# Modulation chunks ahead of the experts: four sets, each adding into one PSUM bank, and the second layer's experts behind the read-back

## The chip, the core and the metric

The kernel runs on one core of one Trainium2 chip. The metric is the device time in microseconds (us). All data is float32. Weights lie in HBM (main memory) and come over the core's 16 DMA engines.

## What is computed

Two layers over 384 tokens of 1024 elements (128 context tokens, 256 latent tokens), cut to what matters:

```python
for l in range(2):
    # 6 vectors of 1024 elements for each of two conditioning vectors (c_ctx, c)
    sh1, sc1, g1, sh2, sc2, g2 = (silu(cond) @ ada_w[l] + ada_b[l]).split(6)   # ada_w[l]: 1024 x 6144
    h = rms_norm(x, norm_mix_g[l]) * (1 + sc1) + sh1
    x = x + g1 * (attention(h) if l == 0 else multi_scale_pool(h))
    h = rms_norm(x, norm_ffn_g[l]) * (1 + sc2) + sh2
    x = x + g2 * moe(h)        # 32 experts, 2 for each token; 3 MB of weights each
```

The six modulation vectors of a layer depend on the conditioning vectors alone, not on x: `ada_w` can be multiplied at any time. It is 24 MB a layer, 48 MB in all. The experts are 96 MB a layer.

## The kernel before

**Engines and queues.** Each engine runs a list of instructions in the order in which it is written, and waits on semaphores. SP (SyncE) issues nearly all loads, in order: a wait on SP holds back every load behind it. PE multiplies, ACT and DVE move results out of PSUM (8 banks of 128 x 512 floats, the accumulators of PE), POOL gathers and scatters token rows with indirect DMAs.

**Modulation.** `ada_w` comes as 24 chunks of 2 MB, 12 a layer, each for 512 of a layer's 6144 columns. For a chunk i, `ada(i)` (line 1254) multiplies the two conditioning vectors by it, in 8 matmuls of 32 stationary columns and 512 moving ones (line 1266), four beside each other in the array; the result stands as rows in bank i % 2. `ada_copy(i)` (ACT, line 634) copies the bank to `adas`. `ada_vectors(i)` (PE, line 1270) turns these rows into columns with 4 small matmuls (line 1276) into bank 2, from where DVE's `modulation` adds the bias and makes the scales. So each chunk costs PE a product, and a turn that needs a copy between. Chunks 0 to 3 come at the head, 4 to 9 between the nine qkv products (line 1342), 10 to 15 (`LATE`) around the router of layer 0, 16 to 19 (`BETWEEN`) after the experts of layer 0, 20 to 23 around the router of layer 1.

**Attention** (lines 1373 to 1440) runs in 28 steps over 24 units. In step u PE makes the scores of unit u (1382), at some steps the product with the values of four units (1399), and the transposes of the probabilities of unit u - 2 (1410, 1417), which wait until DVE has copied those of unit u - 3; ACT takes exponentials (687), DVE the row maxima (949), the scaling (958) and the copies (968). From step 19 on the output projection (1438) runs along.

**Router and experts.** `norm_pe` (1455), the router's logits (1474), the tokens turned to rows (1493), and a long chain of small DVE instructions with small matmuls between, which ends in two tables: the first (1537) gives the indices by which POOL gathers rows, the second (1550) the weights. Then 32 tiles of 64 rows run, one for each expert, and in layer 0 one more tile for an expert with more rows. `rows_T` (1571), `gate_up` (1595), `hidden_T` (1604) and `down` (1619) are PE's work of a tile. The weights of four experts have a place in `ring`, those of a fifth (`more_gu`, `more_down`) in other buffers. The load for a later expert into a place waits until the tile that held it is through (`gu_mm`, `down_mm`). After the last tile of layer 0 its results are read back from HBM (503), added to x, pooled and multiplied (1691, 1731), and layer 1 goes on with its norm and router.

**Places of chunks.** Three places (TAIL, LEFT, RIGHT) are used in turn, two more are where `wo` goes later (HIGH0, HIGH1). Chunks 16 to 23 use places of the ring as well, so the experts of layer 1 are loaded as these chunks are multiplied. LEFT and RIGHT lie in `adaw`, whose first part is the tiles' gathered rows: POOL clears it (line 531) when chunk 14 is multiplied.

Of the kernel before, what the change touches and what calls it, by code (L numbers as in the profile page):

```python
# [26 lines left out]
ALU = mybir.AluOpType  # L27
# [3 lines left out]
P = 128  # L31
# [27 lines left out]
for _name, _w in (("ident", P), ("ones", P), ("upper", P), ("sel2", 2), ("assign", 6), ("eps", 1), ("column_sum", 1),  # L59
# [11 lines left out]
def constants():  # L71
# [10 lines left out]
    put("sel2", (p % 32) == np.arange(2)[None, :])  # L82
# [50 lines left out]
def build(nc, x_prompt, x_sample, c, cache_k, cache_v, c_ctx, norm_mix_g, norm_ffn_g, ada_w, ada_b,  # L133
# [3 lines left out]
    with ExitStack() as ctx:  # L137
# [19 lines left out]
        condT = sb("condT", [P, KD, 32])  # L157
# [40 lines left out]
        ada_place += [ring[:, 0, 0:KD * ACH], ring[:, 1, 0:KD * ACH]]  # L198
        TAIL, LEFT, RIGHT, HIGH0, HIGH1, SLOT0, SLOT1, SPLIT = range(8)
        ADA_AT = [TAIL, LEFT, RIGHT, HIGH0, HIGH1] + [(i + 2) % 3 for i in range(5, 16)]  # L200
        ADA_AT += [SLOT0, SLOT1, RIGHT, SPLIT, HIGH0, HIGH1, RIGHT, RIGHT]
# [36 lines left out]
        split = [xT[:, :, :].rearrange("p k t -> p (k t)"), flat_h[:, 2 * D:3 * D]]  # L238

        def ada_weights(i):  # L240
            if ADA_AT[i] == SPLIT:
                return [split[k // 6][:, k % 6 * ACH:(k % 6 + 1) * ACH] for k in range(KD)]
            return [ada_place[ADA_AT[i]][:, k * ACH:(k + 1) * ACH] for k in range(KD)]

# [15 lines left out]
        s_adaw = [sem(f"s_adaw{i}") for i in range(8)]  # L260
# [72 lines left out]
        LATE = AFTER_QKV[6] + 1  # L333
        BETWEEN = LATE + 6
# [8 lines left out]
        MODS_STEP = 5  # L343
        WO_STEPS = {19 + d: d for d in range(KD)}
        WO_BANKS = (2, 7)
# [14 lines left out]
        def ada_bank(i):  # L360

            return bank[i % 2]

# [7 lines left out]
        def _(sp):  # L371
            def load_ada(i):
                if ADA_PRIOR[i] >= 0:
                    sp.wait_ge(ada_mm, ADA_PRIOR[i] + 1)
                w = ada_w[i // NCH, i % NCH]
                if ADA_AT[i] == SPLIT:
                    sp.dma_start(split[0], w[:, 0:6 * ACH]).then_inc(s_adaw[SPLIT], 16)
                    sp.dma_start(split[1], w[:, 6 * ACH:]).then_inc(s_adaw[SPLIT], 16)
                else:
                    sp.dma_start(ada_place[ADA_AT[i]], w).then_inc(s_adaw[ADA_AT[i]], 16)  # L380
# [1391 lines left out]
```

## Time and profile before

| | |
|---|---|
| median of 3 runs | 904.78 us (903.8 to 907.23) |
| the profiled execution | 905.74 us, of which 903.7 us are its span, first to last instruction |
| PE busy | 751.9 us (83%) |
| DVE, ACT, POOL busy | 356.5, 151.8, 174.9 us |
| chunk products (line 1266) | 208 matmul rows, 28.4 us busy on PE in all |
| moved from HBM | 294.35 MB, mean 326 GB/s |
| granted TensorE clock | 0.937 of 2.4 GHz on average |

The page of the profile splits the span in 40 slices of 22.6 us and gives for each the busy share of every engine in tenths, the granted clock of PE and the share of the DMA engines. The chain is the work that ended last, followed back from the end. In the timeline the number in brackets is how long the engine sat idle before a row, and what ended it. A matmul on float32 is two passes, so 8 matmuls stand as x16.

### The profile page before, as it was taken

The numbers are of one execution on the slowest core, as the hardware profiler recorded it, in microseconds if no ns is written. First come the engines' busy times: TensorE is split into PE (matmuls) and PEld (weight loads), VectorE is DVE, ScalarE is ACT, GpSimd is POOL, SyncE is SP. The second block draws the span as 40 slices with busy tenths as digits, with TensorE's granted clock in tenths as the row PEclk, the third lists the DMA queues.
The fourth block names the chain that finished last, engine by engine and source line by source line (L and its number), as shares of the span: only waits on it lengthen the run. The fifth ranks groups of instructions, "written<-read, shape, count | busy, mean of one in ns | idle before, by whom it ended". The sixth has DMA issues, their size and how long they took to land.

```text
span 903.7 us, 13190 instructions
## 1 busy us (share of the span) xinstructions
PE 751.9 (83%) x4704; PEld 425.8 (47%) x4704; DVE 356.5 (39%) x834; ACT 151.8 (17%) x360; POOL 174.9 (19%) x275
## 2 busy tenths in 40 slices
PE   4999977899889999877787885986999988877860
PEld 3544543478456554444444534544655544444430
DVE  2221448732463434333333334455244423333333
ACT  3211155520431100000000013442010000000000
POOL 0000400000003333322333210002134333322220
PEclk9999969999989999999999988985999999999995
DMA  9998700005886999999999988986599999999925
GB/s 345 428 433 378 211 1 12 1 1 232 354 318 265 386 410 418 422 422 419 422 421 420 389 373 326 387 341 253 213 403 378 423 422 422 420 424 421 414 91 209
DMA packets 39384, 294.35 MB, mean 326 GB/s; under 512 B 10584, under 2 KB 12048, under 8 KB 19376
## 3 DMA queue, kind: packets, MB, share of 16 engines
q1 hardware_dynamic: 26656, 275.50, 74.4%
q0 software_dynamic: 10880, 13.26, 4.8%
q10 hardware_dynamic: 1808, 5.06, 1.4%
q8 instruction: 25, 0.41, 0.2%
q14 instruction: 15, 0.12, 0.0%
HBM read 293.23 MB, written 22.02 MB: 349 GB/s over the span
## 4 chain that ended last, share of the span: by engine, by line
PE 59%; DMA 28%; DVE 6%; issue 3%; ACT 2%; SPq 1%; POOL 0%; ACTq 0%; POOLq 0%; DVEq 0%
DMA ring<-in_moe_w_in 22%; PE bank L1595 18%; PE bank L1619 8%; PE bank L1342 7%; PE bank L1266 4%; PE bank L1438 3%; PE bank L1571 3%; PE bank L1276 2%; DMA adaw<-results 2%; PE bank L1446 2%; PE bank L1474 2%; PE bank L1399 1%; PE bank L1455 1%; DMA adaw<-in_ada_w 1%; PE bank L1731 1%
## 5 line engine op out<-in xcount | busy, mean ns | idle before, releaser
L1595 PE MATMUL bank<-ring,qkv 128*64 128x256 f32 x2016 | 247.0, 399 | 61.1 <-issue 39.1
L1595 PEld LDWEIGHTS bank<-ring,qkv 128*64 128x64 f32 x2016 | 161.0, 143 | 129.3 <-issue 70.4
L1121 DVE COPY qkv<-bank 128x512 f32<-128x512 f32 x64 | 44.3, 692 | 224.7 <-PE bank L1571 224.7
L553 POOL DMA_INDIRECT results<-adaw,scur x65 | 67.6, 1040 | 315.0 <-DVE adaw L1144 280.3
L1619 PE MATMUL bank<-ring,qkv 128*64 128x512 f32 x504 | 122.0, 604 | 1.2 <-DVE qkv L1133 0.8
L816 ACT ACTIVATE qkv<-bank 128x128 f32<-128x128 f32 x64 | 17.8, 278 | 441.6 <-PE bank L1595 441.6
L543 POOL DMA_INDIRECT adaw<-rows,gcur x57 | 59.1, 1036 | 44.3 <-POOL gcur L540 44.3
L1342 PE MATMUL bank<-ring,hT 128*128 128x512 f32 x144 | 63.7, 596 | 1.3 <-DVE hT L891 1.3
L1619 PEld LDWEIGHTS bank<-ring,qkv 128*64 128x64 f32 x504 | 31.0, 136 | 47.5 <-issue 45.6
L1144 DVE SCALAR_TENSOR_TENSOR adaw<-bank,wcur,adaw 128x512 f32<-128x512 f32 x64 | 48.1, 751 | 2.3
L1142 DVE SCALAR_TENSOR_TENSOR adaw<-qkv,wcur 128x512 f32<-128x512 f32 x64 | 48.1, 751 | 2.3
L1133 DVE COPY qkv<-bank 128x128 f32<-128x128 f32 x64 | 18.7, 292 | 76.7 <-PE bank L1604 76.7
L1571 PE MATMUL bank<-con,adaw 128*128 128x128 f32 x260 | 43.1, 289 | 5.1 <-DMA adaw<-rows,gidx 3.2
L1342 PEld LDWEIGHTS bank<-ring,hT 128*128 128x128 f32 x144 | 26.7, 190 | 32.8 <-issue 31.6
L1571 PEld LDWEIGHTS bank<-con,adaw 128*128 128x128 f32 x260 | 27.6, 142 | 30.0 <-issue 30.0
L531 POOL MEMSET adaw<- 128x2048 f32 x2 | 3.6, 1804 | 194.3 <-PE bank L1266 161.8
L1604 PEld LDWEIGHTS bank<-con,qkv 128*128 128x128 f32 x64 | 9.0, 141 | 52.7 <-DVE qkv L1127 51.1
L1266 PE MATMUL bank<-adaw,condT 128*32 128x512 f32 x208 | 28.4, 669 | 2.5 <-DMA adaw<-in_ada_w 2.5
L1276 PEld LDWEIGHTS bank<-con,adas 128*128 128x128 f32 x192 | 23.1, 192 | 13.9 <-issue 13.9
L687 ACT ACTIVATE ring<-bank,ss 128x384 f32<-128x384 f32 (+1 forms) x48 | 24.0, 506 | 32.3 <-DVE ss L949 32.2
L1438 PE MATMUL bank<-hT,ring 128*128 128x256 f32 x128 | 29.1, 380 | 0.0
L1438 PEld LDWEIGHTS bank<-hT,ring 128*128 128x128 f32 x128 | 23.7, 190 | 3.7 <-DVE xT L979 0.8
(231 smaller groups left out, 764.0 us busy)
## 6 DMA issues: line engine op xcount, KB each, us to landing
ring<-in_moe_w_in SPq DMA_DIRECT2D x63, 2048.0 KB, 24.5
ring<-in_moe_w_out SPq DMA_DIRECT2D x63, 1024.0 KB, 20.4
adaw<-in_ada_w SPq DMA_DIRECT2D x13, 2048.0 KB, 18.2
ring<-in_ada_w SPq DMA_DIRECT2D x10, 2048.0 KB, 20.9
ring<-in_attn_w_qkv SPq DMA_DIRECT2D x3, 2048.0 KB, 35.7
ring<-in_attn_w_o SPq DMA_DIRECT2D x1, 4096.0 KB, 22.9
adaw<-in_moe_w_in SPq DMA_DIRECT2D x2, 2048.0 KB, 7.8
adaw<-results SPq DMA_DIRECT2D x8, 512.0 KB, 6.1
```

The source lines that it names most:

```text
L543: pool.indirect_dma_start(xg[:, b], None, rows, bass.IndirectOffsetOnAxis(ap=gcur[:, b:b + 1], axis=0), bounds_check=row_limit, oob_is_err ...
L553: pool.indirect_dma_start(res, bass.IndirectOffsetOnAxis(ap=scur[:, p, :], axis=0), yout[:, p], None, bounds_check=res_limit, oob_is_err=F ...
L1121: V.tensor_copy(xgT[:, p], bank[2][:, :]).then_inc(xgT_ready, 1)
L1142: V.scalar_tensor_tensor(yout[:, p], gdiff, wcur[:, p, 1:2], glat, ALU.mult, ALU.add).then_inc(y_order, 1)
L1144: V.scalar_tensor_tensor(yout[:, p], bank[4 + p % 2][:, :], wcur[:, p, 0:1], yout[:, p], ALU.mult, ALU.mult)\
L1266: last = T.matmul(out[32 * j:32 * j + 32, :], condT[:, k, :], w[k], start=half == 0, stop=half == 1, skip_group_check=True)
L1276: last = T.matmul(bank[2][:, at:at + 2], adas[:, i % 4, j * P:(j + 1) * P], C("sel2"), start=True, stop=True)
L1342: last = T.matmul(bank[5 + g % 3][:, :], hT[:, k, t * P:(t + 1) * P], wqkv[n][:, k, :], start=k == 0, stop=k == KD - 1)
L1438: last = T.matmul(bank[WO_BANKS[d % 2]][:, 0:NTOK - CTX], wo[:, k, d * P:(d + 1) * P], hT[:, k, CTX:NTOK], start=k == 0, stop=k == KD - 1)
L1571: last = T.transpose(bank[2][:, i * P:(i + 1) * P], xg[:, q, i * P:(i + 1) * P], ident)
L1595: last = T.matmul(bank[p][64 * a:64 * a + 64, 0:2 * P], xk[:, k % 4, k // 4], w[:, :, k, a * P:(a + 1) * P], start=k == 0, stop=k == KD - ...
L1619: last = T.matmul(bank[4 + p][64 * a:64 * a + 64, :], hidT[:, p, 64 * j:64 * j + 64], w[j][:, a * 512:(a + 1) * 512], start=j == 0, stop=j ...
```

## The change

- The 24 chunks are cut into four sets, `SETS = (0, 4, 10, 19, 24)`. All chunks of a set add into one bank: the two conditioning columns stand in columns 30 and 31 of a buffer 62 wide that is otherwise zero, and chunk number m of a set multiplies the 32 columns from 30 - 2m on, so its result lands in rows 2m and 2m + 1 and the other rows add zero. One copy and one group of 4 turning matmuls then serve a whole set (`set_copy`, `vectors`) in place of one for each chunk.
- Chunk 10 moves to just ahead of attention, chunks 11 to 18 into attention at steps 2, 3, 4, 5, 9, 12, 13 and 16 (`ADA_STEPS`), each between the scores and the transposes. Chunks 19 to 23 stay around the router of layer 0. No chunk is left in layer 1, nor between the layers.
- SP loads chunks 8 to 21 in one row as places come free, and 22 and 23 behind the third expert of layer 0. After layer 0 it issues the read-back at once, and behind it the four ring experts of layer 1 with no wait between.
- POOL clears `adaw` when chunk 20 is multiplied. `modulation` and the scales are split; `MODS_STEP` is 4 instead of 5; the two banks of the output projection change places, and its second product waits for `set_copy(2)`.

```diff
+        ADA_AT = [TAIL, LEFT, RIGHT, HIGH0, HIGH1] + [(i + 2) % 3 for i in range(5, 22)] + [TAIL, RIGHT]
...
+        SETS = (0, 4, 10, 19, 2 * NCH)
+        SET_BANK, VECTOR_BANK = (0, 1, 2, 0), (2, 0, 2, 2)
...
+        ADA_STEPS = {2: 11, 3: 12, 4: 13, 5: 14, 9: 15, 12: 16, 13: 17, 16: 18}
...
-        MODS_STEP = 5
+        MODS_STEP = 4
...
-            for i in range(8, LATE + 3):
+            for i in range(8, 22):
                 load_ada(i)
...
-                    for i in range(LATE + 3, BETWEEN):
-                        load_ada(i)
-                    sp.wait_ge(ada_mm, LATE + 4)
+                    load_ada(22)
+                    load_ada(23)
+                    sp.wait_ge(ada_mm, 23)
                     load_expert(l, 3)
...
                     sp.wait_ge(extras_over, 1)
-                    load_ada(BETWEEN + 4)
-                    load_ada(BETWEEN + 5)
-                    for b in range(2):
-                        sp.wait_ge(ada_mm, BETWEEN + b + 1)
+                    for b in range(RING):
                         load_expert(l, b)
                     sp.wait_ge(x_sum, TT)
-                    load_ada(BETWEEN + 6)
-                    sp.wait_ge(ada_mm, BETWEEN + 6)
-                    load_expert(l, 2)
-                    load_expert(l, 3)
-                    load_ada(BETWEEN + 7)
-                    sp.wait_ge(ada_mm, 2 * NCH)
-                    sp.wait_ge(ada_vec, 2 * NCH - 2)
...
-                    pool.wait_ge(ada_mm, BETWEEN - 1)
+                    pool.wait_ge(ada_mm, 21)
...
+            def set_copy(n):
+
+                act.wait_ge(ada_mm, SETS[n + 1])
+                A.activation(adas[:, n, :], bank[SET_BANK[n]][:, :], ACT.Copy).then_inc(ada_copied, 1)
...
             def ada(i):
 
+                n = set_of(i)
+                c = 30 - 2 * (i - SETS[n])
...
-                        last = T.matmul(out[32 * j:32 * j + 32, :], condT[:, k, :], w[k],
-                                        start=half == 0, stop=half == 1, skip_group_check=True)
+                        last = T.matmul(out[32 * j:32 * j + 32, :], condT[:, k, c:c + 32], w[:, k],
+                                        start=i == SETS[n] and half == 0, stop=i + 1 == SETS[n + 1] and half == 1,
+                                        skip_group_check=True)
...
+            def vectors(n):
+
+                pe.wait_ge(ada_copied, n + 1)
+                a, b = SETS[n], SETS[n + 1]
+                out = bank[VECTOR_BANK[n]][:, 8 * a:8 * b].rearrange("p (c j x) -> p j c x", j=4, x=2)
+                for j in range(4):
+                    last = T.matmul(out[:, j], adas[:, n, j * P:(j + 1) * P],
+                                    C("sel")[:, 0:2 * (b - a)].rearrange("p (c x) -> p c x", x=2), start=True, stop=True)
                 last.then_inc(ada_vec, 1)
...
+            vectors(1)
+            ada(10)
             pe.wait_ge(qk_copied, 4)
             pe.wait_ge(k_copied, 3)
-            pe.wait_ge(ada_copied, LATE)
...
+                if u in ADA_STEPS:
+                    ada(ADA_STEPS[u])
...
-                    ada(LATE)
-                    ada(LATE + 1)
-                else:
-                    ada(BETWEEN + 4)
-                    ada(BETWEEN + 5)
-                    ada_vectors(BETWEEN + 4)
-                    ada_vectors(BETWEEN + 5)
+                    vectors(2)
+                    ada(19)
+                    ada(20)
...
-                    ada(BETWEEN)
-                    ada(BETWEEN + 1)
-                    ada_vectors(BETWEEN)
-                    ada_vectors(BETWEEN + 1)
-                    ada(BETWEEN + 2)
-                    ada(BETWEEN + 3)
                     pe.wait_ge(mods_ready, 4)
-                    ada_vectors(BETWEEN + 2)
-                    ada_vectors(BETWEEN + 3)
```

How the instructions move. On PE, from a qkv product to the first attention steps, the kernel before has (1266 is a chunk product, 1276 its turn, 1328 the turns of queries and keys, 1382 scores, 1410 and 1417 transposes):

```order
L1342 MATMUL bank<-ring,hT 128x512 x8
L1266 MATMUL bank<-adaw,condT 32x512 x8
L1276 MATMUL bank<-con,adas 128x2 x4
L1328 MATMUL bank<-con,qkv 128x128 x8
L1342 MATMUL bank<-ring,hT 128x512 x8
L1276 MATMUL bank<-con,adas 128x2 x4
L1342 MATMUL bank<-ring,hT 128x512 x8
L1328 MATMUL bank<-con,qkv 128x128 x2
L1328 MATMUL bank<-con,ring 128x128 x2
L1328 MATMUL bank<-con,qkv 128x128 x10
L1382 MATMUL bank<-ring 128x384 x6
L1410 MATMUL bank<-con,ring 128x128 x4
```

The same place in the changed kernel, where line 1216 is the chunk product, 1227 the turn of a set, 1291 the qkv product, 1277 the turns of queries and keys, 1331 the scores:

```order
L1291 MATMUL bank<-ring,hT 128x512 x8
L1216 MATMUL bank<-adaw,condT 32x512 x8
L1277 MATMUL bank<-con,qkv 128x128 x8
L1291 MATMUL bank<-ring,hT 128x512 x16
L1277 MATMUL bank<-con,qkv 128x128 x2
L1277 MATMUL bank<-con,ring 128x128 x2
L1277 MATMUL bank<-con,qkv 128x128 x10
L1227 MATMUL bank<-con,adas 128x6x2 x4
L1216 MATMUL bank<-ring,condT 32x512 x8
L1331 MATMUL bank<-ring 128x384 x6
L1216 MATMUL bank<-adaw,condT 32x512 x8
L1361 MATMUL bank<-con,ring 128x128 x4
```

The turns between the qkv products are gone; one turn and chunk 10 stand ahead of the first scores, and a chunk between scores and transposes. On PE, from the norm of layer 1 (1455) to the first tile (1571), the kernel before has:

```order
L1455 MATMUL bank<-qkv,con 128x384 x8
L1266 MATMUL bank<-ring,condT 32x512 x16
L1276 MATMUL bank<-con,adas 128x2 x8
L1474 MATMUL bank<-hT,wr 36x384 x8
L1478 MATMUL bank<-con,rt 128x36 x3
L1266 MATMUL bank<-adaw,condT 32x512 x8
L1493 MATMUL bank<-con,hT 128x128 x16
...
L1276 MATMUL bank<-con,adas 128x2 x4
L1537 MATMUL bank<-hT 128x43 x6
L1276 MATMUL bank<-con,adas 128x2 x4
L1550 MATMUL bank<-hT 128x43 x6
L1571 MATMUL bank<-con,adaw 128x128 x4
```

The changed kernel there (1407 is its norm, 1422 its logits, 1477 and 1484 its tables, 1507 its first rows):

```order
L1407 MATMUL bank<-qkv,con 128x384 x8
L1422 MATMUL bank<-hT,wr 36x384 x8
L1426 MATMUL bank<-con,rt 128x36 x3
L1437 MATMUL bank<-con,hT 128x128 x16
...
L1477 MATMUL bank<-hT 128x43 x6
L1484 MATMUL bank<-hT 128x43 x6
L1507 MATMUL bank<-con,adaw 128x128 x4
```

All four chunks and their turns have left this place. On SP, around the read-back (503), the kernel before issues:

```order
L380 DMA ring<-in_ada_w 128x4096
L380 DMA adaw<-in_ada_w 128x4096
L377 DMA xT<-in_ada_w 128x3072
L378 DMA hT<-in_ada_w 128x1024
L503 DMA adaw<-results 128x1024 x4
L503 DMA qkv<-results 128x1024 x2
L380 DMA ring<-in_ada_w 128x4096 x2
L383 DMA ring<-in_moe_w_in 128x4096
L387 DMA ring<-in_moe_w_out 128x2048
```

and the changed one, where line 467 is the read-back and 370 and 374 are the expert loads:

```order
L467 DMA adaw<-results 128x1024 x4
L467 DMA qkv<-results 128x1024 x2
L370 DMA ring<-in_moe_w_in 128x4096
L374 DMA ring<-in_moe_w_out 128x2048
L370 DMA ring<-in_moe_w_in 128x4096
```

The chunk loads ahead of and behind the read-back are gone, and the expert loads follow it.

## Rows read from the trace of the kernel before

**Rows 1.** The page, 40 slices: granted PE clock and DMA share in tenths

```profile
PEclk9999969999989999999999988985999999999995
DMA  9998700005886999999999988986599999999925
```

**Rows 2.** Window of layer 0's tiles: length; busy PE, PEld, DVE, ACT, POOL; clock, DMA, GB/s

```profile
352.00:520.00 168.00, 136.11 (x939) 77.07 (x937) 57.41 (x124) 5.66 (x21) 50.26 (x82) 0.98 1.01 417
```

**Rows 3.** The chain that ended last, head and qkv products: start, length, what

```profile
33.43 1.89 PE bank L1276 x16
...
59.52 1.85 PE bank L1266 x16
61.37 0.98 PE bank L1276 x8
...
69.33 1.85 PE bank L1266 x16
```

**Rows 4.** The chain, attention: first exponential, first values, first output projection

```profile
126.42 1.24 ACT ring L687 x4
...
143.84 2.93 PE bank L1399 x12
...
182.11 3.52 PE bank L1438 x16
```

**Rows 5.** Timeline of PE in attention: start, length, idle before it in brackets

```profile
130.76 1.65 PE L1382 MATMUL bank<-ring 64*128 64x384 f32 x4
...
135.80 0.92 PE L1382 MATMUL bank<-ring 64*128 64x384 f32 x4
...
174.67 0.63 PE L1410 MATMUL bank<-con,ring 128*128 128x128 f32 x4 [1.38 <-DVE ring L968]
```

**Rows 6.** Windows, columns as in the window above

```profile
160.00:182.00 22.00, 17.85 (x107) 9.39 (x105) 16.72 (x42) 13.45 (x46) 0.00 (x0) 1.00 0.00 1
585.00:591.00 6.00, 5.62 (x49) 2.80 (x48) 3.35 (x4) 1.72 (x3) 0.00 (x0) 1.00 0.30 68
592.00:602.00 10.00, 8.62 (x23) 2.70 (x27) 5.46 (x17) 5.15 (x9) 0.00 (x0) 0.69 1.01 430
```

**Rows 7.** The chain, layer 0 from its last norm product to its first tile

```profile
234.42 1.58 PE bank L1455 x4
...
241.18 5.82 PE bank L1474 x16
...
264.27 2.79 PE bank L1537 x12
267.06 3.57 PE bank L1266 x16
...
276.72 0.47 PE bank L1571 x4
```

**Rows 8.** The chain, last scatter of layer 0, then that of layer 1

```profile
540.03 6.25 DMA results<-adaw,scur
...
877.43 2.83 DMA results<-adaw,scur
```

**Rows 9.** The chain, layer 1 from its norm to its first tile

```profile
585.18 3.57 PE bank L1266 x32
...
592.80 8.00 PE bank L1474 x16
...
603.65 11.04 DMA adaw<-in_ada_w
...
619.57 1.39 PE bank L1537 x12
...
622.57 6.62 DMA adaw<-rows,gidx
```

**Rows 10.** DMA issues: count, median us from issue to landing

```profile
adaw<-rows,gidx POOLq DMA_INDIRECT x8, 3.8
```

**Rows 11.** Timeline of DVE, router of layer 1: what the first table waits for

```profile
616.90 1.62 DVE L1073 TENSOR_SCALAR hT<-con,rt 128x128 f32<-128x128 f32 x6
```

More of the change, by code:

```diff
@@ L197, in build @@
                      high[:, 0:KD * ACH], high[:, KD * ACH:KD * D]]
[L198 to L201, printed above, removed]
+        TAIL, LEFT, RIGHT, HIGH0, HIGH1 = range(5)
+        ADA_AT = [TAIL, LEFT, RIGHT, HIGH0, HIGH1] + [(i + 2) % 3 for i in range(5, 22)] + [TAIL, RIGHT]
         ADA_USE = [ADA_AT[:i + 1].count(ADA_AT[i]) for i in range(2 * NCH)]
@@ L235, in build, with set_of @@
         flat_h = hT[:, :, :].rearrange("p k t -> p (k t)")
[L238 to L243, printed above, removed]
+        SETS = (0, 4, 10, 19, 2 * NCH)
+        SET_BANK, VECTOR_BANK = (0, 1, 2, 0), (2, 0, 2, 2)
+        def set_of(i):
+            return sum(i >= first for first in SETS) - 1
         more_gu = cc[:, 4096:8192]
@@ L259, in build @@
         s_wqkv = [sem(f"s_wqkv{n}") for n in range(3)]
-        s_adaw = [sem(f"s_adaw{i}") for i in range(8)]
+        s_adaw = [sem(f"s_adaw{i}") for i in range(5)]
         pool_order, dve_order = sem("pool_order"), sem("dve_order")
@@ L620, in _ @@
             for i in range(2):
[L621 removed]
+                A.activation(condT[:, :, 30 + i], gains[:, 40 + 8 * i:48 + 8 * i], ACT.Silu).then_inc(cond_ready, 1)
             act.wait_ge(s_const, 16)
@@ L757, in raw @@
                             .then_inc(xt_copied, 1)
-                    for i in range(BETWEEN, BETWEEN + 4):
-                        ada_copy(i)
                     square(0)
@@ L807, in keep @@
                     A.activation(xtok[:, t, q * 512:(q + 1) * 512], bank[6 + n % 2][:, :], ACT.Copy).then_inc(x1_copied, 1)
-                for i in (range(LATE + 3, BETWEEN) if l == 0 else (BETWEEN + 7,)):
-                    ada_copy(i)
+                if l == 0:
+                    set_copy(3)
                 def silu(s, p, old=True):
@@ L870, in _, with modulation, scales @@
             dve.wait_ge(rows_read, 3)
[L872 to L874 removed]
+            def modulation(n, l, a, b):
+                cols = bank[VECTOR_BANK[n]][:, l * 2 * NMOD + 2 * a * KD:l * 2 * NMOD + 2 * b * KD]
                 m = mods[:, l, a * KD:b * KD, :]
[L876 to L886 removed]
+                order(V.tensor_tensor(m, cols.rearrange("p (m c) -> p m c", c=2),
+                                      bias[:, l, a * KD:b * KD].unsqueeze(2).to_broadcast([P, (b - a) * KD, 2]), ALU.add))
+            def scales(l, i, first):
+                m = mods[:, l, i * KD:(i + 1) * KD, :]
+                order(V.tensor_scalar(m, m, 1.0, None, ALU.add))
+                order(V.tensor_tensor(m, m, gains[:, first:first + KD].unsqueeze(2).to_broadcast([P, KD, 2]), ALU.mult))
+            dve.wait_ge(ada_vec, 1)
+            modulation(0, 0, 0, 2)
+            scales(0, 1, 0)
             V.memset(ss[:, 15:16], 0.0).then_inc(mods_ready, 1)
@@ L972, in _ @@
                 if u == MODS_STEP:
-                    dve.wait_ge(ada_vec, LATE)
-                    modulation(0, 2, 5)
+                    dve.wait_ge(ada_vec, 2)
+                    modulation(1, 0, 2, 5)
+                    scales(0, 4, 16)
                     V.memset(ss[:, 16:17], 0.0).then_inc(mods_ready, 1)
```

157 lines of the change are left out of this document (42 added, 115 removed).

## The prediction

> **What bounds the kernel now.** I read the page first: PE's clock and the DMA share in 40 slices [rows 1]. The DMA engines stand at 9 tenths in the two long stretches of expert tiles and at 0 from 113 to 203 us, which is attention. The window over most of layer 0's tiles [rows 2] shows 1.01 of DMA share at 417 GB/s, with PE busy 136 of 168 us: the tiles are bound by weights. Five experts are loaded ahead in each layer, the load of the sixth waits for the first tile's gate_up, and from there 27 experts of 3 MB follow each other. So the end of a stretch of tiles is the start of its first gate_up plus a fixed stream, and the change leaves this stream as it is. What can change the time lies outside: the head, qkv, attention, the two routers, and the passage between the layers. The 16 MB that layer 1 no longer loads are worth nothing by themselves, since its five experts wait loaded for the first tile in both kernels. I went through the chain in these parts, then the timelines for what stands beside it. All times below are against the profiled execution, 905.74 us with a span of 903.7; its run is 0.96 above the median of 904.78.
>
> **Head and qkv.** At the head the chunks' turns go from four groups to one. PE's chunks, transposes of x and turns stand end to end; in the order of the new kernel one turn of 0.98 is left behind chunk 3 and its copy. By the old rows the two last groups took 1.89 [rows 3], an earlier one 0.98; against this the last copy is now exposed for 0.7 or so. I take 1.8 off (bounds 0, if the first qkv weights land no earlier than now, and 2.2). Between the qkv products six turns of 0.98 go: the pitch from one chunk to the next is 9.81, of which the chunk is 1.85 and the turn 0.98 [rows 3], and what is left is the product. That is 5.9 off, as long as chunk loads keep up; the DMA share falls under 9 tenths from the fourth slice on, 68 us [rows 1], so the queue runs dry while the products go on. Sum: 7.7 earlier at the end of qkv. A rule of the Trainium skill speaks against the moves further on (TensorEngine Tiling, Key Properties): changing the tiling mode drains TensorE, and each chunk in attention adds two changes between 32-column and full matmuls. The row leaves nothing for it here: 59.52 + 1.85 = 61.37 and 61.37 + 0.98 = 62.35, to the hundredth the next start. By the rule each of 16 changes would cost something; by the row the sum is unchanged.
>
> **Ahead of attention.** One turn and chunk 10 now stand between the last transposes of keys and the first scores, with nothing to hide them. The clock is at its half level there: scores of one unit took 1.65 at 130.76 and 0.92 at 135.80 [rows 5]. A chunk takes 1.85 at full and 3.57 at half clock [rows 3, 7]. I take 1.1 + 3.6 = 4.7. As PE is then busy without a break from the transposes on, I expect the full clock back by the first scores, so that they take half as long and the first exponential comes 5.0 earlier than the old 126.42 [rows 4], a loss of 2.7 of the 7.7 (bounds 1.0 and 4.7).
>
> **Chunks 11 to 14** (steps 2 to 5). The old kernel takes 17.4 from the first exponential to the first product with values at 143.84 [rows 4], partly at half clock, and with a pause in PE while DVE normalizes the context queries at step 3. At full clock a step with a chunk is 0.92 of scores, 1.85, and about 0.8 of transposes (0.63 and the third key tile's [rows 5]), 3.6 in all. After 1.2 of exponential and 0.9 of scores three such steps take 10.8, and DVE, which by then is in its normalization, needs about 5 more for that and two steps: 17.9. A chunk of 2 MB takes 5 us at 417 GB/s [rows 2] and some to start, so chunk 14, whose place is free only after chunk 11, would be just in time. With some of it at half clock I take a loss of 1.5 (bounds 0 and 7).
>
> **Chunks 15 to 18.** Here PE is busy 17.85 of 22 us with three of the chunks to come, 5.6 us of work [rows 6], so at least 1.4 is lost there if every gap serves. Gaps ahead of transposes like the 1.38 at 174.67 [rows 5] do serve: there PE waits for DVE's copy. Step by step I find 0.8 for chunk 15, 1.5 for 16 and 17, 0.4 for 18: 2.7 (bounds 1.4 and 7.4). The output projection, at 182.11 in the old chain [rows 4], then starts at -7.7 + 2.7 + 1.5 + 2.7 = **-0.8** against before. If all ends sit at their bounds, -5.7 and +13.2.
>
> **Router of layer 0.** The two chunks and the one turn behind the norm are hidden as now, under 5.2 us of DVE and ACT from 236.00 to 241.18 [rows 7]. One turn on each side of chunk 21 goes, but DVE's marks bound the counting matmuls: 1.25 earlier. The first table comes at 263.0 instead of 264.27 and takes 2.79 at half clock [rows 7]. Then one chunk of up to 3.57, the second table of 1.39 to 2.79 [rows 7, 9], one turn of 1.0, and 0.5 of DVE; old: two chunks and four turns. First rows at 272.4 to 273.8 for the old 276.72 [rows 7]. POOL's clearing, which the old kernel could only do after chunk 14, is out of the way; the gather lands by 271 at its median of 3.8 [rows 10]. I take **-3.4** (bounds -2.2 and -4.8).
>
> **Between the layers.** The last scatter of layer 0 takes 6.25 with four chunk loads in the queues, that of layer 1, with no load about, 2.83 [rows 8]. The read-back is issued behind it, so **-3.4** (bounds 0 and -3.8). The chunks between hid under scatter and read-back and cost nothing; their products kept PE at work, though, see below. I add **+0.5** for a longer stay at half clock.
>
> **Layer 1.** From the last norm product, 585.18, to the logits at 592.80 are 7.6 [rows 9]; in layer 0 the same norm takes 5.2, as there DVE has no modulation to wait for. So -2.4. The wait of 11.04 for a chunk's weights [rows 9] looks like the big gain and is not: the first table at 619.57 needs DVE's six marks, the last of which ends at 618.52 [rows 9, 11]. Only the 1.05 between go, and about 1.3 of matmuls at half clock may; against this the table itself may take 2.79 instead of 1.39. I take -0.8. The gather of 6.62 [rows 9] runs against the fifth expert's load, which now comes long before: 3.8 by its median [rows 10], -2.8. Together **-6.0** (bounds -3.5 and -7.8). The tiles and the tail follow unchanged.
>
> **Sum.** -0.8 - 3.4 - 3.4 + 0.5 - 6.0 = -13.1: 905.74 - 13.1 = 892.6 for the profiled execution, and 0.96 less for the median, **891.7 us**.
>
> **Rivals.**
> - *Attention pays each chunk in full* (chance 0.12). For it: PE is the busiest engine there, 17.85 of 22 [rows 6]. Against: the gaps. Price: 8 x 1.85 = 14.8 and 4.7 ahead, so -7.7 + 4.7 + 14.8 = +11.8 at the output projection, 12.6 more than forecast: 904.3, no change.
> - *Half clock through attention* (0.04): slower. The place is steps 2 to 16. For it: in 585 to 591 PE was busy 5.62 of 6 us, all chunks and turns, and yet the stretch from 592 ran at 0.69 [rows 6], so chunks may not hold the clock. Against: in 160 to 182 it was 1.00 [rows 6], with the same scores and transposes. Price: 8 x 3.57 = 28.6 and 4.7, so +25.6, 26.4 more than forecast: 918. It decides where the loss ahead of and in attention is over 24.5 (the 7.7 before it, the 12.3 behind it, and 4.5): less 4.7, that is 2.5 for each chunk.
> - *PE cold behind the read-back* (0.12). Without chunks PE rests some 16 us, and the window products, pool products and logits start at half clock; the logits already took 8.00 instead of 5.82 [rows 7, 9]. The logits lost 2.2 by it; if the window and pool products, each of such a length, lose as much and half as much again, the passage is 6.6 longer: 898.3. The Trainium skill puts it as a rule (TensorE: Matmul & The Clock Gate, The HAM clock gate): the throttled state is the default, and activity releases it. Against: 5 us after a product at half clock the next was at full [rows 5].
> - *Everything serves* (0.14): the chunks keep the clock full in attention and sit in gaps (-3.5 at the output projection), routers at their far bounds (-4.8, -7.8), scatter -3.8: -19.9 and 0.96, 884.9.
> - *The forecast* has 0.58.
>
> **Numbers.** The kernel's runs spread 0.4%, so 0.5%, 4.5 us, is about what can be told from no change. Slower by more needs over 909.3: the half clock, and a loss in attention with one at layer 1 beside it, 0.05. Within: 900.3 to 909.3, most of the first rival and a third of the cold-PE case, 0.13. Faster: 0.82. The range: below 884 nothing but the far bounds together, above 900 the first two rivals, so 884 to 900 leaves out about 0.2.
>
> **What would show it.** Chain: output projection within 3 us of 182; first layer-0 gate_up near 274; last scatter of layer 0 under 3.5 us; logits of layer 1 at 5.2 us behind the norm; its first gather near 4; no idle PE on chunk weights in attention. Total time of the two tile stretches equal to before. The prediction is wrong if attention grows over 15 us, if a chunk load is late at steps 4 to 9, or if the tiles of either layer take longer because their loads now start otherwise.

## The result, and the profile after

The changed kernel takes 893.0 us (median of 4 executions, 889.83 to 893.44), the kernel before beside it 906.0 (median of 4): a ratio of 0.985, 95% interval 0.9816 to 0.9884. Forecast were 891.7 us and "faster" with 0.82. In a second round of runs it was 891.3 against 902.8 (0.9877, 0.9851 to 0.9903). The profiled execution of after is the fastest, 889.83, so the two profiled ones differ by 15.9 and the medians by 13.0; where the other 3 may lie is said below.

The page of after: busy times, granted clock and DMA share, as in [rows 1].

```profile
PE 726.6 (82%) x4544; PEld 404.4 (46%) x4544; DVE 356.0 (40%) x830; ACT 140.8 (16%) x340; POOL 175.4 (20%) x275
...
PEclk9999999999977999999999996985999999999995
DMA  9999858714868899999999947923699999999935
```

The chain that ended last, with the places of [rows 3, 4]:

```profile
3.70 27.67 DMA ring<-in_ada_w
31.41 1.97 PE bank L1216 x16
...
59.33 1.85 PE bank L1216 x16
61.18 7.06 PE bank L1291 x16
68.25 1.85 PE bank L1216 x16
...
116.76 3.51 PE bank L1216 x16
120.27 0.87 PE bank L1331 x4
...
122.16 1.24 ACT ring L648 x4
...
140.08 2.80 PE bank L1350 x12
...
180.65 3.46 PE bank L1390 x16
```

Each matmul stands as two rows (x16 for 8); that these are its two passes, as said ahead, no run shows. The turn between chunk and product is gone: the pitch is 8.92 for 9.81. The first two rows are why the head gave nothing: the load ahead of chunk 3 lands at 31.37 and the chunk is multiplied at once, so what went from TensorE before that had lain under the load. Chunk 10, at 116.76, runs at half clock, the scores behind it at full. The output projection starts 1.46 earlier than in [rows 4].

The same chain from layer 0's norm to its first tile, for [rows 7]:

```profile
232.89 1.58 PE bank L1407 x4
...
240.94 5.34 PE bank L1422 x16
...
252.81 2.45 PE bank L1446 x12
...
264.70 2.79 PE bank L1477 x12
...
276.34 3.67 PE bank L1531 x15
```

The norm ends 1.5 earlier than before, the logits (240.94) start 0.24 earlier and the first table 0.43 later. Two windows say why. First VectorE and GpSimd there (start, length, engine, line):

```profile
239.17 1.63 DVE L960 TENSOR_SCALAR hT<-hT,mods 128x128 f32<-128x128 f32 x1
239.43 1.37 DVE L958 TENSOR_TENSOR hT<-xT,qkv 128x384 f32<-128x384 f32 x1
239.89 0.97 DVE L960 TENSOR_SCALAR hT<-hT,mods 128x128 f32<-128x128 f32 x1
```

```profile
238.91 1.80 POOL L495 MEMSET adaw<- 128x2048 f32 x1 [133.76 <-PE bank L1216]
```

GpSimd clears xg as soon as chunk 20 is multiplied, and VectorE's steps beside it take 1.63 and 1.37 in place of 0.34 and 0.55. All end with it: 240.80, 240.80 and 240.86 for 240.71. Before, the clearing ran at 270.72. Then windows, with the columns of [rows 6] (the granted clock is the third number from the end):

```profile
248.00:252.00 4.00, 3.07 (x27) 1.74 (x20) 3.48 (x17) 1.93 (x2) 0.00 (x0) 1.00 0.49 123
252.00:256.00 4.00, 3.52 (x24) 3.20 (x22) 0.94 (x6) 1.92 (x2) 0.00 (x0) 0.65 1.06 390
256.00:260.00 4.00, 4.00 (x22) 2.35 (x24) 1.28 (x7) 2.86 (x3) 0.00 (x0) 0.50 0.79 313
```

TensorE is at 0.65 in the window from 252 and at its half level behind it, and the counts at 252.81 take 2.45 (1.53 at the full level, in a run below). The kernel before had the full level there, and up to 260:

```profile
252.00:256.00 4.00, 3.08 (x27) 2.60 (x25) 1.33 (x6) 3.31 (x4) 0.00 (x0) 1.00 0.76 299
```

Between the layers and in layer 1, for [rows 8, 9]:

```profile
534.30 2.37 DMA results<-adaw,scur
...
538.51 6.78 DMA adaw<-results
...
548.55 2.61 PE bank L1619 x10
...
575.14 1.57 PE bank L1407 x4
...
581.91 8.21 PE bank L1422 x16
...
607.71 2.80 PE bank L1477 x12
...
617.43 4.75 PE bank L1531 x21
```

The scatter takes 2.37 for 6.25, the logits stand 5.2 behind the norm for 7.6, the gather is no longer in the chain, and layer 1's first tile starts 13.8 earlier (617.43 for 631.26).

### The profile page after: what moved, and what is told of

It is laid out like the page before. It is cut to its first block, busy times and chain, and to the rows that moved or that the text cites. A ratio compares the mean times of both kernels' runs of the same rounds, so it can differ in the third digit from the quotient of the medians.

```text
span 887.8 us, 12796 instructions
## 1 busy us (share of the span) xinstructions
PE 726.6 (82%) x4544; PEld 404.4 (46%) x4544; DVE 356.0 (40%) x830; ACT 140.8 (16%) x340; POOL 175.4 (20%) x275
## 4 chain that ended last, share of the span: by engine, by line
PE 57%; DMA 28%; DVE 7%; issue 4%; SPq 1%; ACT 1%; POOL 0%; POOLq 0%; DVEq 0%
DMA ring<-in_moe_w_in 22%; PE bank L1531 17%; PE bank L1555 8%; PE bank L1291 7%; PE bank L1216 3%; PE bank L1390 3%; DMA ring<-in_ada_w 3%; PE bank L1507 3%; DMA adaw<-results 2%; PE bank L1398 2%; PE bank L1422 2%; PE bank L1350 1%; PE bank L1331 1%; PE bank L1407 1%; PE bank L1659 1%
## 5 line engine op out<-in xcount | busy, mean ns | idle before, releaser
L1531 PE MATMUL bank<-ring,qkv 128*64 128x256 f32 x2016 | 241.5, 393 | 63.1 <-issue 39.7
L1531 PEld LDWEIGHTS bank<-ring,qkv 128*64 128x64 f32 x2016 | 157.1, 141 | 129.7 <-issue 66.6
L1555 PEld LDWEIGHTS bank<-ring,qkv 128*64 128x64 f32 x504 | 31.0, 136 | 47.5 <-issue 45.6
L1291 PEld LDWEIGHTS bank<-ring,hT 128*128 128x128 f32 x144 | 26.8, 190 | 36.7 <-issue 35.5
L1216 PE MATMUL bank<-adaw,condT 128*32 128x512 f32 x240 | 30.2, 623 | 0.0
L1540 PE MATMUL bank<-con,qkv 128*128 128x128 f32 x64 | 21.2, 331 | 2.0 <-DVE qkv L1083 2.0
## 6 DMA issues: line engine op xcount, KB each, us to landing
adaw<-in_ada_w SPq DMA_DIRECT2D x15, 2048.0 KB, 11.6
```

The costliest lines, as they stand in the source:

```text
L1216: last = T.matmul(out[32 * j:32 * j + 32, :], condT[:, k, c:c + 32], w[:, k], start=i == SETS[n] and half == 0, stop=i + 1 == SETS[n + 1] ...
L1291: last = T.matmul(bank[5 + g % 3][:, :], hT[:, k, t * P:(t + 1) * P], wqkv[n][:, k, :], start=k == 0, stop=k == KD - 1)
L1531: last = T.matmul(bank[p][64 * a:64 * a + 64, 0:2 * P], xk[:, k % 4, k // 4], w[:, :, k, a * P:(a + 1) * P], start=k == 0, stop=k == KD - ...
L1540: T.transpose(bank[3][:, 0:P], hid[:, p], ident).then_inc(hid_mm, 1)
L1555: last = T.matmul(bank[4 + p][64 * a:64 * a + 64, :], hidT[:, p, 64 * j:64 * j + 64], w[j][:, a * 512:(a + 1) * 512], start=j == 0, stop=j ...
```

## The experiments

All are edits of the changed kernel. My theory A was: the gain is the six turns in qkv, the scatter and read-back without chunk loads, and layer 1's norm and gather; layer 0's router gave nothing because of the clearing and the clock. The rivals stand in each expectation. Ratios are to the kernel before, run beside each.

**The clearing, later** (`e1_clear_late`)

```diff
                     pool.wait_ge(s_out, 32)
+                    pool.wait_ge(slots_ready, 6)
```

> The changed kernel, with GpSimd's clearing of xg in layer 0 (1.80 us at 238.91 in its profile, beside the norm's VectorE work) held until the first six masks of the router are ready (about 264.5), where VectorE waits for TensorE's table. Theory A, the clearing slows VectorE's norm: the rstd step falls from 1.37 to about 0.6 us and the step behind it from 0.97 to 0.35, the logits start 1.2 to 1.4 earlier against the end of the norm's products (now 6.45 behind them), and the time is 1 to 1.4 us shorter. Rival B, the logits are late because of the set's vectors and chunks 19 and 20 ahead of them on TensorE: nothing moves, within 0.3 us. Rival C, the late clearing delays the first gather of layer 0: the first product of layer 0 starts up to 1.8 us later and the time is 0.5 to 2 us longer.

Measured: 890.8 us, 0.9839 (0.981 to 0.9868). Of its chain:

```profile
232.55 1.58 PE bank L1408 x4
...
239.31 5.82 PE bank L1423 x16
...
263.04 2.79 PE bank L1478 x12
```

The logits stand 5.18 behind the end of the norm's products for 6.47, so 1.3 came back as A says. This holds in every profile: 6.5 in all six with the clearing beside the norm, 5.2 in all six with it elsewhere. But a VectorE step of three elements a partition now stands beside the clearing, which ran from 263.13 to 264.93:

```profile
263.09 1.87 DVE L1033 TENSOR_SCALAR rt<-rt 128x3 f32<-128x3 f32 x1
```

That hides under the table's 2.79. From the table to the first tile it takes 12.28 for 11.64, with the set's turns at 1.45 for 1.30 and chunk 23 at 3.57 for 3.24; but with the clearing early this stretch took 11.26 to 13.3 in six profiles, so the 0.6 is not shown to be the clearing's. The first tile starts 0.7 earlier, counted from the first qkv product, in place of 1.3, and 0.3 earlier than in the second profile of the changed kernel. In the time of the kernel that is not to be told from nothing.

**Six groups of turns back between the qkv products** (`e2_turns_back`)

```diff
+                if g - 1 in AFTER_QKV:
+                    for j in range(4):
+                        T.matmul(bank[0][:, 400:402], adas[:, 0, j * P:(j + 1) * P], C("sel")[:, 0:2], start=True, stop=True)
```

> The changed kernel, with a group of four matrix products of 128x128 weights by two columns put back behind each of six query, key and value products, where the kernel before had the chunks' turns (they write a spare place, so nothing else changes). Theory A, the turns themselves cost what the query, key and value stage gave: that stage's end moves from 111.65 to 116.7 to 117.3, the time is 5.0 to 5.9 us longer. Rival B, that stage follows the landing of its loads and the turns were beside it: under 1 us longer. Rival C, half of the price lay in the copy from PSUM that each turn waited for: 2 to 4 us longer, since here no copy is waited for.

Measured: 898.1 us, 0.992 (0.9895 to 0.9944), 7.3 above the run with the late clearing beside it (up to 1.3 of this can be that clearing). Of its chain:

```profile
70.47 1.85 PE bank L1216 x16
72.32 0.98 PE bank L1303 x8
73.31 6.97 PE bank L1291 x16
80.28 1.85 PE bank L1216 x16
...
123.45 1.85 PE bank L1216 x16
...
127.19 1.24 ACT ring L648 x4
```

The pitch is 9.81 again, to the hundredth that of [rows 3], with no copy waited for: A holds, and B and C fall. The end of qkv is 6.7 later (118.3). Of that 5.35 are the six turns. The rest is mostly a stretch at a lower clock in the first products, ahead of the first of these turns: the first two groups of products took 15.67 for 13.97, with 0.67 granted from 38 to 42. Such a stretch comes and goes with the execution: from the first product to the end of qkv, 75.2 us passed in both profiles of the changed kernel and in three of the variants, and 76.9 to 78.1 in six others with the same code up to there. Unexpected: chunk 10 took 1.85, not 3.51, so only 5.0 is left at the first exponential. What the time has beyond that can be such variation too: layer 0's last gate product took 5.38 here and 3.70 in the changed kernel.

**The eight chunks in attention over 64 of 512 columns** (`e3_narrow_chunks`; it leaves out the rest of their product)

```diff
+                cols = 64 if 11 <= i < 19 else ACH
...
-                        last = T.matmul(out[32 * j:32 * j + 32, :], condT[:, k, c:c + 32], w[:, k],
+                        last = T.matmul(out[32 * j:32 * j + 32, 0:cols], condT[:, k, c:c + 32], w[:, k, 0:cols],
```

> The changed kernel, with the eight chunks inside the attention (11 to 18) multiplied over 64 of their 512 columns only (it leaves out the rest of their product, so layer 1's modulation is not the reference's); their loads stay. From the first exponential to the output projection it took 58.3 us in both profiles of the changed kernel. Theory A, the eight chunks cost the attention 2.3 to 3.5 us and the rest of their 14.8 us is hidden: that stretch takes 54.8 to 56. Rival B, they are all on the path: it takes 45 to 47. Rival C, they are all hidden, and what the attention lost is the clock at its start: it stays at 58. The first exponential itself stays where it is in all three, since chunk 10 is whole.

Measured: 894.3 us, 0.9844 (0.9806 to 0.9883), not faster. From the first exponential to the output projection 57.5 us pass for 58.5. Windows and timeline of this execution:

```profile
130.00:140.00 10.00, 7.25 (x98) 3.98 (x96) 9.76 (x19) 4.06 (x15) 0.00 (x0) 1.00 1.00 411
140.00:150.00 10.00, 8.19 (x28) 3.29 (x28) 5.85 (x17) 4.06 (x14) 0.00 (x0) 0.66 1.01 433
```

```profile
139.51 0.43 PE L1217 MATMUL bank<-adaw,condT 128*32 128x64 f32 x16 [2.20 <-DMA adaw<-in_ada_w]
```

A narrow chunk takes 0.43, so eight give back 11.4 us of TensorE, and the stretch gives 1.0. Other bounds take over: chunk 14 waits 2.20 for its load, VectorE is busy 9.76 of 10, and behind that wait the clock stands at 0.66 (1.00 in the same ten us of the changed kernel, counted from the first exponential), so that the first values product takes 4.81 for 2.80. With these 2.0 taken off, the chunks cost 3.0, inside A's range, but that is worked out and not seen: of the three, the run rules out only B. What it shows by itself is that removing most of the chunks' work won 1.0 us here and nothing that the time of the kernel shows. Against the expectation the first exponential moved too, 13.15 behind qkv for 10.54, in code that the edit leaves alone.

**Layer 1's fifth expert as late as before** (`e4_fifth_late`)

```diff
                     sp.wait_ge(x_sum, TT)
+                    sp.wait_ge(tab_mm, 3)
```

> The changed kernel, with the fifth expert's load of layer 1 held until the first table is multiplied, about where the kernel before issued it, so that it lands beside the first gather. Theory A, the gather was slow because of this load: it takes 6 to 7 us again from its issue to landing, the first product of layer 1 is 2 to 3 us later, and so is the end. Rival B, the gather is shorter in the changed kernel since there are no chunk loads and turns around it: under 0.5 us. Rival C, the later load is itself late for its tile (the fifth), as the queue has nothing ahead: up to 4 us more than A, with a wait for s_more in the fifth tile.

Measured: 894.0 us, 0.9894 (0.9864 to 0.9925), 3.2 above the run with the late clearing beside it, which again can hold up to 1.3 of that clearing. Of its chain:

```profile
611.87 6.70 DMA adaw<-rows,gidx
...
620.64 5.75 PE bank L1532 x32
```

The gather is 6.70, as the 6.62 of [rows 9], and the first tile starts at 620.64 for 617.43. In the changed kernel the gather is issued at 612.12 and the rows are multiplied at 615.70 without a wait, so there it took at most 3.6. A holds: the fifth expert's load makes the gather slow, with no chunk about.

**Chunk loads back ahead of the read-back** (`e5_loads_ahead`, and the same kernel again, `e5_ahead_again`, for its trace)

```diff
+                if l == 0:
+                    sp.wait_ge(gu_mm, LAST[0] + 1)
+                    sp.dma_start(ring[:, 0, 0:KD * ACH], ada_w[1, 8]).then_inc(s_ahead[0], 16)
...
+                    sp.dma_start(ada_place[RIGHT], ada_w[1, 10]).then_inc(s_ahead[2], 16)
...
+                    for n in range(3):
+                        sp.wait_ge(s_ahead[n], USED[n] + 16)
                 sp.wait_ge(results_in, l + 1)
```

> The changed kernel, with four chunk-sized loads put back ahead of the read-back of layer 0, at the places and behind the waits that the kernel before had, and multiplied by nobody. The read-back waits for three of them. Theory A, the last scatter and the read-back were slow because of these loads: the last scatter takes 5.5 to 6.5 us again in place of 2.37, the first window product is 3.5 to 5 us later, and the time is 3.5 to 5 us longer. Rival B, the scatter was slow in one execution only: under 1 us. Rival C, what cost the time before was the four chunks' products and their turns ahead of the windows on TensorE: then the loads alone give under 1.5 us.

> The kernel with four chunk-sized loads put back ahead of the read-back, again, for its trace. Its time was 896.3 us before. Theory A, scatter and read-back are slowed by the loads: last scatter 5.5 to 6.5 us in place of 2.4, the first window product 3 to 5 us later after the end of layer 0's tiles. Rival B, the scatter is short and the tiles of layer 0 are longer instead, as their own weights share the queue: tiles of layer 0 from first gate product to their end over 256 us in place of 255.3.

Measured: 896.3 us (0.9904, 0.9872 to 0.9936) and 895.6 us (0.992, 0.9895 to 0.9945), the second 4.3 above the changed kernel beside it. Of its chain:

```profile
538.08 7.03 DMA results<-adaw,scur
...
547.00 7.04 DMA adaw<-results
...
557.30 2.60 PE bank L1635 x10
```

The scatter alone is 4.6 longer than the 2.38 of the changed kernel beside it, above the 5.5 to 6.5 of A. Layer 0's tiles are not longer (255.9 for 255.6). A holds without any product: the loads did it.

**The changed kernel again** (`e0_after_again`)

> The changed kernel as it is, once more, on the chip and beside the runs of the kernels that follow, as what they are to be held against. Both theories: 890 to 894 us, and in its profile the same places as in the first: the clearing of xg at about 239 slows two of the norm's VectorE steps, the last scatter of layer 0 takes about 2.4 us, the first gather of layer 1 lands in about 3.8, chunk 10 ahead of the attention runs at the half clock (3.5 us).

Measured: 891.3 us, 0.9877. The places are the same: the norm's step beside the clearing takes 1.55, chunk 10 3.5, the scatter 2.38.

**The routers' idle gaps filled** (`e8_router_filled`). Its warm(n) issues n products of 128 columns of constants into a bank that nobody reads; `e7_all_filled` adds those for the read-back and ahead of attention. The clearing is late in both, and their distance to the changed kernel holds that too.

```diff
+                if l == 1:
+                    warm(18)
...
+                warm((2, 8)[l])
                 pe.wait_ge(picked, l + 1)
...
+                warm((12, 16)[l])
                 pe.wait_ge(slots_ready, l * 12 + 6)
...
+                warm((0, 8)[l])
                 pe.wait_ge(slots_ready, l * 12 + 12)
```

> The changed kernel with the clearing of xg late in layer 0 (as in the run with that alone) and with spare matrix products of 128 columns in TensorE's idle gaps around the routers of both layers: behind the norm's products of layer 1 (18), ahead of the counts (2 and 8), ahead of the first table (12 and 16) and between the tables of layer 1 (8). They write a bank that nobody reads. Theory A, these stages run at the half clock because TensorE had idled in them: layer 1's logits take 5.4 in place of 8.2 us, the tables 1.4 in place of 2.8, and the time is 4 to 7 us below the changed kernel's. Rival B, the chain through them is VectorE's and the products' clock hardly counts: under 2 us. Rival C, the spare products are themselves in the way where the clock does not rise: the first table of either layer waits for them, 2 to 6 us longer.

> As the kernel with the routers' gaps filled, and also with 56 spare products in the wait for layer 0's read-back and 8 in the waits ahead of the attention. Theory A, chunk 10 runs at the full clock (1.85 in place of 3.5 us) and the first exponential is 1.6 us sooner, the window products and what follows them gain 1 to 2 us more, and the time is 2 to 4 us below that of the kernel with the routers' gaps filled. Rival B, window products wait for VectorE's scaling and ScalarE, not the clock: under 1 us from the read-back part. Rival C, the spare products raise the activity of TensorE so far that the clock falls somewhere else, in the attention or the tiles: no gain or a loss.

> The kernel with all gaps filled, again, beside the next one. Both theories: 877 to 883 us, first window product 3.1 us behind the read-back's last landing, with 4.4 us of idle TensorE ahead of it and the window products that follow at a clock below the full one.

Measured: 884.0 us, 0.9784 (0.9749 to 0.9818), with the routers filled; 879.9, 0.974 (0.9714 to 0.9766), and 880.8, 0.9713 (0.9694 to 0.9732), with all filled. Layer 1 with the routers filled, on TensorE (idle before it in brackets):

```profile
586.24 5.80 PE L1429 MATMUL bank<-hT,wr 128*36 128x384 f32 x16 [1.18 <-DVE hT L961]
...
598.59 1.53 PE L1454 MATMUL bank<-rt,con 128*128 128x32 f32 x12 [0.56 <-DVE rt L993]
...
601.91 3.84 PE L1412 MATMUL bank<-con 128*128 128x128 f32 x32
608.20 1.53 PE L1486 MATMUL bank<-hT 128*128 128x43 f32 x12 [2.45 <-DVE hT L1026]
...
615.84 2.38 PE L1541 MATMUL bank<-ring,qkv 128*64 128x256 f32 x20 [0.85 <-DVE qkv L1078]
```

From layer 1's logits to its first tile pass 29.6 us for 35.5, and in layer 0 32.5 for 35.4. A holds for the routers: 7.4 us under the changed kernel's 891.3, just over its 4 to 7, with single executions from 879.1 to 889.5. The table takes 1.53 for 2.79 and the logits 5.80 for 8.21 (6.86 in the changed kernel's second profile). Filling the other gaps gives 4.1 more, of which 1.65 is seen: chunk 10 takes 1.85, and the first exponential follows qkv by 8.9 for 10.5. The read-back's part is not shown to pay. In the first of the two profiles the clock was 0.78 from 546 to 550 and the pooled products followed the first window product by 11.1 (11.6 in the changed kernel), in the second the clock was full and they followed by 9.9. But the scatter was slower beside the spare products, 3.25 and 2.89 for 2.38, and from layer 0's last product to layer 1's clearing pass 39.5 and 37.4 us, for 39.0 and 38.5 in the changed kernel's two profiles.

**The wait ahead of the window, and the clearing in VectorE's gap** (`e10_window_filled`: 24 products for 8; `e11_clear_in_gap`: also the clearing elsewhere)

```diff
-                    warm(8)
+                    warm(24)
...
-                    pool.wait_ge(slots_ready, 6)
+                    pool.wait_ge(h_ctx, KD)
```

> As the kernel with all gaps filled, with 24 spare products in place of 8 behind the landing of the first part of the read-back, which fills the 4.4 us ahead of the first window product. Theory A, the window products (2.08 and 1.91 us for the first two groups) then take 1.8 and 1.1 us at the full clock, 1 us is gained up to the pooled products, and the time is 0.5 to 1.2 us less. Rival B, the window products wait for VectorE's scaling, which waits for ScalarE: the pooled products start at the same distance (11.1 us) from the first window product. Rival C, the spare products run over the first window's data by up to 1 us: 0.5 to 1 us longer.

> As the kernel with all gaps and the window filled, with the clearing of xg in layer 0 behind the last VectorE step of the norm (h_ctx at eight) in place of behind the router's masks. There VectorE is idle for 2.33 us (242.34 to 244.67 in the kernel before this one), and the clearing takes 1.81; behind the masks, a VectorE step of three elements a partition (0.17 us elsewhere) took 1.88 beside it. Theory A, any VectorE step beside the clearing waits for it: in the new place none does, that step takes 0.17 again, the first product of layer 0 follows the logits' start by 31.1 us in place of 32.8, and the time is 1 to 1.7 us below 878.8. Rival B, the first gather, not that step, sets the start of the tiles: 0 to 0.5 us. Rival C, the clearing slows ScalarE's or VectorE's reading of the logits instead: 1 us longer than A.

Measured: 878.8 us, 0.9689 (0.9669 to 0.9709), and 878.6, 0.9715 (0.9682 to 0.9748). The pooled products follow the first window product by 9.88 in the first, and by as much in the kernel without it, run beside it (11.1 in that one's earlier profile), so its share is not shown. In the second the clearing, 246.32 to 248.12, stands in VectorE's gap, and no step is slow beside it, but from logits to first tile 32.4 pass for 32.8: 0.4 of the 1.7 that A gives. The table took 2.09 there for 1.53 and chunk 23 2.92 for 1.85, at a lower clock: the second table, which had waited 1.49 for VectorE in the run before, now stood right behind that chunk. Both are the best seen: by the ratios 1.4 to 1.9 per cent under the changed kernel, on the way to which the products and the clearing are not told apart.

## Why the forecast held, and where its steps did not

The time is 1.3 above the forecast, inside its range. By the profiled pair, one execution of each kernel, step by step:

- **Head**: forecast -1.8, measured -0.2. The bound of 0 that I named came true: chunk 3's load lands at 31.37, and the turns that went had stood beside it. In three other profiles with the same code up to there, the first qkv product started at 37.6 to 38.0 for 36.44.
- **Qkv**: -5.9, measured -5.35: 0.89 for each turn, not 0.98, as a product behind a chunk takes 7.06 and one behind a turn 6.97. The turns' run shows the cause.
- **Ahead of attention**: a loss of 2.7, measured 1.3. Chunk 10 took 3.51, as taken; the scores behind it had the full clock. In three other profiles with the same code up to there the first exponential followed qkv by 12.1 to 13.2 in place of 10.5, a loss of 2.8 to 3.9: the 1.3 is that of one execution.
- **Chunks 11 to 14**: 1.5, measured 0.5 (17.92 from the first exponential to the first values product for 17.42). **Chunks 15 to 18**: 2.7, measured 2.3. By the narrow chunks the two cost 3.0 together, an estimate (above), for the 2.8 measured.
- **Output projection**: -0.8, measured -1.5.
- **Router of layer 0**: -3.4, measured -0.2. This step failed. "POOL's clearing, which the old kernel could only do after chunk 14, is out of the way" was half the truth: it had moved from behind the tables to beside the norm, where VectorE is on the path, and cost 1.3 (shown by the run with it late). The kernel before had shown such a hold already, at a place off the chain:

```profile
270.72 1.80 POOL L531 MEMSET adaw<- 128x2048 f32 x1 [161.82 <-PE bank L1266]
271.02 1.52 DVE L1101 TENSOR_SCALAR rt<-rt 1x11 f32<-1x11 f32 x1
```

  This step takes 0.29 in the changed kernel, with no clearing beside it. And I let the clock be half only at the table: it fell 11 us sooner, and with filled gaps logits to table take 22.0 for 23.8, 1.8. That the turns which went had held it up before is likely and not shown. The two make 3.1 of the missing 3.2 in the profiled execution; from the first table to the first gate product 11.64 pass for 13.76, as forecast. Over all profiles of the changed kernel and its variants, the logits start 34.4 to 37.5 us ahead of the first gate product in the seven without spare products (36.85 before) and 32.4 to 33.3 in the five with them, so the loss by the clock is shown and its place and size differ between executions. The terms named for the first rows add up to 272.25 to 273.65, not 272.4 to 273.8, which changes nothing.
- **Between the layers**: -3.4 and +0.5, measured -6.8. The scatter gave 3.9 for 3.4, and the loads' run shows the cause; the read-back and the window took back 1.1 for 0.5. The other 4.0 I did not forecast: the stretch from the first tile to the end of layer 0 was 255.3 for 259.4, of which 2.9 is one gate product at its end, 6.56 in the profile of before, at a granted clock of 0.50 and 0.61, and 3.70 in that of after, at 1.00. It took 3.70 in seven profiles of the changed kernel and its variants and 5.2 to 5.4 in five, with the same code around it, so it goes with the execution's clock. This, or the losses at the head and ahead of attention that this execution of after did not have, can be the 3 by which the profiled pair differs from the medians; none is shown to be.
- **Layer 1**: -6.0, measured -5.4: logits -2.4 as forecast, and the gather, which the fifth expert's run gives 3.2 (forecast 2.8). The table took 2.80, as allowed for, for 1.39.
- **Tiles of layer 1**: 0, measured 0 (235.4 both). The final read-back was 1.7 shorter (8.02 for 9.73) and the scatter ahead of it 0.4; over all profiles that read-back takes 7.4 to 9.9, so this is no gain of the change that the runs show.

Of the rivals, "attention pays each chunk in full" and "half clock through attention" fell by the profile. "PE cold behind the read-back" was there in kind: the clock is half from 537 to 553, but from the first window product to the norm's end 28.1 us pass for 27.7, so it cost 0.4 there in place of 6.6. The sum came out right by errors of both signs: +3.2 in the router, +1.6 at the head, against -3.9 between the layers, of which 2.9 lie in a product that the change doesn't touch, -2.8 in and ahead of attention and -2.1 in the tail; qkv and layer 1 are small.

On the rule of the Trainium skill that the prediction weighed, a drain at each change of the tiling mode (TensorEngine Tiling, Key Properties), the rows decide less than the forecast took from them. They stand end to end as before, 116.76 + 3.51 = 120.27, the next start. But the ends of matmul rows are modelled, so such time could lie inside a row. The narrow chunks bound it: 64 columns take 0.43 and 512 take 1.92 in the same view, and by a line through the two 0.22 does not go with the columns. That is an estimate of at most 1.7 us for the eight chunks in attention, whatever it is made of.

## What to carry to other kernels

When an edit removes a wait, follow what it sets free on every engine: here a clearing by GpSimd was free to run 32 us sooner and cost 1.3 on VectorE, which was on the path; where VectorE idled, no step was slow beside it. Plain loads beside an indirect scatter or gather that gates a stage make it longer (2.38 to 7.03 and at most 3.6 to 6.70 here): put them well before or behind. And read the granted clock in each stage that is bound by short products with idle time between: spare products in the gaps of this kernel, with the clearing held late, were worth as much (11.4 us) as the whole change beside them (11.5).

## What the runs showed of the hardware

- A GpSimd clearing of 128x2048 takes 1.80, and some VectorE steps beside it, however small, end only with it: 1.87 for one of 128x3 that takes 0.17 elsewhere. In all profiles only TENSOR_SCALAR steps on SBUF were held (and what stood behind them). In layer 1 the same clearing, 570.71 to 572.51, ran beside VectorE steps of another form at their usual length:

```profile
570.71 1.80 POOL L495 MEMSET adaw<- 128x2048 f32 x1 [33.57 <-PE bank L1659]
```

```profile
570.69 0.74 DVE L945 SCALAR_TENSOR_TENSOR xT<-bank,mods,xT 128x128 f32<-128x128 f32 x2 [0.55 <-PE bank L1659]
```

The Trainium skill has the rule (SBUF — State Buffer, SBUF: two separate sides): VectorE and GpSimd share a port pair as an exclusive lock, which some forms of VectorE steps need and others don't. The traces agree, with 1.87 for 0.17 on one side and 0.37 a step on the other. Had I asked of the freed clearing which VectorE steps it would meet, the failed step would have had its 1.3.
- With 11 us of TensorE's work removed from attention, ten us there had a granted clock of 0.66 where the changed kernel had 1.00, behind a wait of 2.20 for a load, and the kernel was no faster. Conversely chunk 10, ahead of attention, ran at the full level (1.85 for 3.51) both with 8 spare products in the idle time ahead of it and in the run with turns between the qkv products; why in the latter is open.
- The granted clock differs between executions of the same code: the qkv products took 75.2 us in five profiles and 76.9 to 78.1 in six.
- An indirect scatter of 2.38 us took 7.03 beside chunk loads, and 2.8 to 3.25 in the four profiles in which TensorE had spare products at that time. For the latter no run shows a cause.
